# First operands in halves, half a compression block moved, fused sum and extremum, value pages placed and ordered anew

## The reference

```python
# layer 0: S5 state space mixer (48 groups of 64 complex states); layer 1: native sparse attention (NSA)
h = rmsnorm(x, norm_mix_pre[i])
z = h @ w_in                                          # memory queries are columns of z
mkv = mem @ w_mem_kv[i]                               # prompt's 256 memory tokens; samples have a cache
m = concat(mixer(z), mem_attention(z[..., memory], mkv))
x = x + rmsnorm(m @ w_out[i], norm_mix_post[i])
g, u = split(rmsnorm(x, norm_ffn_pre[i]) @ w_ffn_in[i])
x = x + rmsnorm((silu(g) * u) @ w_ffn_out[i], norm_ffn_post[i])
# S5: abar = exp(lam * dt); bu = ug @ bbar; h = scan(abar, bu); y = gelu(c @ h + d * u); y *= sigmoid(y @ w_glu + b)
# NSA compressed keys and values, for the samples out of 8 x 16 pages of 128 rows:
hid = proj[:, :-1, :, 0] + proj[:, 1:, :, 1] + bias   # two overlapping halves of blocks of 32
ckv = gelu(hid) @ w2
# each branch (compressed, selected blocks, window):
s = q @ k * 0.125 - slope[head] * distance            # masked where distance < 0
o = softmax(s) @ v                                    # o = sum of gate * o over the three branches
```

## Time and profile before

| what | value |
|---|---|
| runs, median (lowest to highest of 3) | 1156.15 us (1154.6 to 1156.6) |
| the profiled execution's own time | 1155.58 us |
| its span, first to last instruction | 1153.9 us |
| mean granted TensorE clock | 0.971 of full speed |
| TensorE, VectorE, ScalarE, GpSimd busy | 1079.0, 364.9, 201.8, 245.1 us |
| moved by transfers | 185.20 MB, mean 160 GB/s |

### The profile page before, as it was taken

How to read it: one execution, slowest core, us unless ns; L and a number is a source line. 1 busy time by engine, 2 the same in 40 slices (tenths; PEclk the granted TensorE clock), 3 DMA queues, 4 the chain that set the end, 5 groups by cost and what they waited for, 6 DMA issues and landing times.

```text
span 1153.9 us, 16960 instructions
## 1 busy us (share of the span) xinstructions
PE 1079.0 (94%) x6364; PEld 790.5 (69%) x6364; DVE 364.9 (32%) x783; ACT 201.8 (17%) x496; POOL 245.1 (21%) x314
## 2 busy tenths in 40 slices
PE   6999999999989999999999999785588999999996
PEld 5766666666767777777786776344466777777774
DVE  5629766630142111100023135895014211110002
ACT  3420001002231000010013132664013100000000
POOL 0608756730001101100000022257300110110000
PEclk9999999999989999999999999897698999999998
DMA  8827333431425656675343246368822444343431
GB/s 324 354 76 259 115 110 114 124 93 37 154 73 183 250 204 224 243 280 201 127 170 128 74 143 197 111 178 314 278 74 74 145 146 133 125 144 101 142 134 66
DMA packets 59118, 185.20 MB, mean 160 GB/s; under 512 B 8609, under 2 KB 39586, under 8 KB 48418
## 3 DMA queue, kind: packets, MB, share of 16 engines
q1 hardware_dynamic: 52322, 165.28, 41.3%
q0 software_dynamic: 6144, 12.59, 3.5%
q10 hardware_dynamic: 576, 6.29, 1.4%
HBM read 180.35 MB, written 10.02 MB: 165 GB/s over the span
## 4 chain that ended last, share of the span: by engine, by line
PE 87%; SPq 6%; issue 3%; DVE 2%; DMA 1%; ACT 0%; DVEq 0%
PE banks L731 30%; PE banks L509 16%; PE banks L771 15%; PE banks L707 15%; SPq L416 3%; PE banks L529 3%; SPq L412 2%; PE banks L677 1%; SPq L395 1%; PE banks L1115 1%; PE banks L690 1%; PE banks L575 1%; PE banks L863 1%; PE banks L484 1%; DMA slabs<-in_w 1%
## 5 line engine op out<-in xcount | busy, mean ns | idle before, releaser
L731 PE MATMUL banks<-normed,slabs 128*128 128x288 f32 x1408 | 347.1, 410 | 9.1 <-ACT normed L1224 9.1
L731 PEld LDWEIGHTS banks<-normed,slabs 128*128 128x128 f32 x1408 | 270.5, 192 | 85.5 <-issue 10.0
L771 PE MATMUL banks<-hidden,slabs 128*128 128x288 f32 x704 | 171.2, 406 | 1.5 <-issue 1.5
L707 PE MATMUL banks<-arena,phase 128*128 128x384 f32 x512 | 170.7, 490 | 0.0
L771 PEld LDWEIGHTS banks<-hidden,slabs 128*128 128x128 f32 x704 | 133.6, 190 | 39.1 <-issue 2.4
L707 PEld LDWEIGHTS banks<-arena,phase 128*128 128x128 f32 x512 | 95.5, 190 | 63.2 <-issue 0.2
L1520 POOL TENSOR_TENSOR projected<-projected,rstd 128x288 f32<-128x288 f32 x44 | 34.9, 793 | 440.8 <-ACT projected L1291 440.8
L509 PE MATMUL banks<-normed,slabs 128*128 128x288 f32 (+1 forms) x416 | 107.7, 411 | 1.2 <-ACT normed L1224 1.2
L509 PEld LDWEIGHTS banks<-normed,slabs 128*128 128x128 f32 (+1 forms) x416 | 75.5, 187 | 26.3 <-ACT normed L1224 3.2
L1606 DVE TENSOR_TENSOR normed<-normed 128x288 f32<-128x288 f32 x24 | 11.0, 459 | 199.0 <-ACT normed L1284 199.0
L1291 ACT ACTIVATE projected<-projected 128x288 f32<-128x288 f32 x44 | 19.5, 443 | 281.4 <-DVE projected L1653 281.4
(11 more groups left out here) (300 smaller groups left out, 1060.9 us busy)
## 6 DMA issues: line engine op xcount, KB each, us to landing
slabs<-in_wfi SPq DMA_DIRECT2D x44, 1024.0 KB, 4.9
slabs<-in_w SPq DMA_DIRECT2D x25, 1024.0 KB, 4.8
arena<-in_cmp SPq DMA_DIRECT2D x128, 192.0 KB, 2.8
slabs<-in_wfo SPq DMA_DIRECT2D x32, 704.0 KB, 4.0
arena<-in_slck POOLq DMA_DIRECT2D x64, 96.0 KB, 3.1
arena<-in_slck SPq DMA_DIRECT2D x64, 96.0 KB, 3.4
out_win_old<-in_winold SPq DMA_DIRECT2D x8, 762.0 KB, 6.4
arena<-in_slcv SPq DMA_DIRECT2D x48, 96.0 KB, 4.2
```

The costliest lines, as they stand in the source:

```text
L707: ins = nc.tensor.matmul(out.rearrange("p h (g s) -> p h g s", s=8), W1S[:, c, a, j, :], PG[b % 2][:, :, c * 8 + j, :, :].rearrange("p g h ...
L731: return nc.tensor.matmul(BK[2 * (u % SLOTS) + c][:, 0:T], wt[:, k, c * P:c * P + P], Hn[:, k, :], start=(k == 0), stop=(k == KC - 1), ski ...
L771: ins = nc.tensor.matmul(BK[b][:, 0:T], wt[:, k, :], HD[:, 11 * kh + k, :], start=(kh + k == 0), stop=(kh * 11 + k == 21))
```

## The change

- **First operands.** The memory tokens and the first slab are issued as two halves each, first halves first and ahead of the constants; TensorE starts on the first halves. VectorE does layer 0's sum of squares, norm and normed tiles ahead of the last three angle steps.
- **Compression.** The last value block is cut: 8 of its products stay, 8 go behind `post_sum(1)`. ScalarE copies the sums in layer 0 and takes their Gelu in layer 1 (`last_hidden`), and `compress_v(7)` goes to `beside_in(10)`. The last `s5_y` stands behind the block.
- **Units.** The prompt's queries are scaled by 0.125 / slope in `in_evac` (two instructions instead of one), so that sum and extremum are one `tensor_tensor_reduce`, with the sign turned. The prompt's compressed scores use the same form, and their own maxima are taken as before.
- **Value pages.** The window's tensors move within `slabs`; sequence 6 goes to `projected`, sequence 7 to `slabs`, half by SP and half by GpSimd, which reads all its 16 numbers. On SP the window values come ahead of the number reads, and the first output slab behind `f = 0`, the others behind `f = 1`.

```diff
 # TensorE
-                compress(b, c, between=lambda i: beside_block(blk, i))
+                compress(b, c, between=lambda i: beside_block(blk, i), products=range(8 if blk == 2 * B - 1 else 16))
...
-                    if n < N_UNIT - 1:
-                        s5_y(n)
+                    s5_y(n)
...
-            compress_v(B - 1)
...
             post_sum(1)
+            compress(B - 1, 1, products=range(8, 16))
             channel_mixer(0)
...
+                if i == 10:
+                    compress_v(B - 1)
...
+                    pe.wait_ge(vpage_loaded[b], 16 * (NPG if b < B - 1 else NPG // 2))
+                if f:
+                    pe.wait_ge(vpage_loaded[B], 16 * NPG // 2)
 # ScalarE
+            def last_hidden(half):
+                key = ("hc", B - 1, 1)
+                if half == 0:
+                    banks.take(act, key)
+                    banks.wait_given(act, ("cv", B - 2))
+                    src = BK[6][:, 0:387].rearrange("p (h n) -> p h n", n=129)[:, :, 1:1 + NCMP]
+                    banks.give(A(HCMP[1].rearrange("p (h n) -> p h n", h=H), src, ACT.Copy), key)
+                else:
+                    banks.wait_given(act, key)
+                    A(HCMP[1], HCMP[1], ACT.Gelu_apprx_tanh, bias=CB[:, 1:2]).then_inc(hid_done, 1)
...
             scaled(2)
+            last_hidden(0)
             channel_mixer(0)
...
                     act.wait_ge(state_stored, 32)
+                    last_hidden(1)
...
-                            ins = A(s, s, ACT.Exp, bias=NM[n % 2][:, j:j + 1], accum_out=RS[n % 2][:, j:j + 1])
+                            ins = A(s, s, ACT.Exp, bias=NM[n % 2][:, j:j + 1], scale=-1.0, accum_out=RS[n % 2][:, j:j + 1])
 # VectorE
+                if m < 6:
+                    dve.wait_ge(cst2_loaded, 16)
+                    ch.step(stt(Z[:, m, 0:TP], src[:, 0:TP], c2("qs")[:, m:m + 1], RST[:, 0:TP], ALU.mult, ALU.mult))
+                    ins = stt(Z[:, m, TP:T], src[:, TP:T], 0.125, RST[:, TP:T], ALU.mult, ALU.mult)
+                elif m < 17:
...
+            sum_squares(0, Z[:, 9, :], [Z[:, 9 + k, :] for k in range(1, KC)])
             shape = [P, SC, SEG]
             dve.wait_ge(cst_loaded, 16)
             ch.step(tt(SIN, U1.unsqueeze(2).to_broadcast(shape), c1("tau").unsqueeze(1).to_broadcast(shape), ALU.mult))
+            dve.wait_ge(x_loaded, 16)
+            inverse_root(0)
+            for k in range(KC):
+                stt(Hn[:, k, :], X[:, k, :], norm_g[:, 0, k:k + 1], RST[:, :], ALU.mult, ALU.mult).then_inc(h_done, 1)
             ch.step(ts(COS, SIN, MAGIC, MAGIC, ALU.add, ALU.subtract))
             ch.step(tt(SIN, SIN, COS, ALU.subtract))
             stt(COS, SIN, 0.25, SIN, ALU.is_gt, ALU.subtract).then_inc(trig_arg, 1)
-            dve.wait_ge(x_loaded, 16)
-            pre_norm(0)
-            for k in range(KC):
-                stt(Hn[:, k, :], X[:, k, :], norm_g[:, 0, k:k + 1], RST[:, :], ALU.mult, ALU.mult).then_inc(h_done, 1)
...
-                            ins = stt(SCP[:, :, hd, :], cd, slopes[hd], v[:, :, h, gg, :], ALU.mult, ALU.add)
+                            n = 6 * par + 2 * h + gg
+                            ins = V.tensor_tensor_reduce(SCP[:, :, hd, :], v[:, :, h, gg, :], cd, slopes[hd], NEG, ALU.add, ALU.max,
+                                                         CMX[:, n:n + 1])
...
-                for par in range(2):
-                    banks.take(dve, ("us", n, par))
-                    banks.give(stt(s[:, par, :], c2("causal"), slopes[4 * h + 2 * gg + par], BK[2 * (n % 2) + par][:, 0:3 * P],
-                                   ALU.mult, ALU.add), ("us", n, par))
-                for par in range(2):
-                    banks.wait_given(dve, ("us", n, par))
-                ch.step(V.tensor_reduce(NM[n % 2][:, 0:2], s[:, :, 0:P], AX_X, ALU.max, negate=True))
-                V.tensor_reduce(NM[n % 2][:, 2:4], s[:, :, P:3 * P], AX_X, ALU.max, negate=True).then_inc(u_max, 1)
+                for t in range(2):
+                    for par in range(2):
+                        if t == 0:
+                            banks.take(dve, ("us", n, par))
+                        a, b = P * t, P * t + P * (t + 1)
+                        ins = V.tensor_tensor_reduce(s[:, par, a:b], BK[2 * (n % 2) + par][:, a:b], c2("causal")[:, a:b],
+                                                     -slopes[4 * h + 2 * gg + par], -NEG, ALU.add, ALU.min,
+                                                     NM[n % 2][:, 2 * t + par:2 * t + par + 1])
+                        if t:
+                            banks.give(ins, ("us", n, par))
+                        else:
+                            ch.tick(ins)
+                    if t == 0:
+                        ch.sync()
 # GpSimd
-            for b in (0, 1, 3, 6):
-                numbers = value_numbers(POOL, b)
+            numbers = [value_numbers(POOL, b) for b in (0, 1, 3)]
+            for b, pages in zip((0, 1, 3), numbers):
                 wait_value_slot(pool, b)
-                load_value_pages(pool, b, numbers)
+                load_value_pages(pool, b, pages)
+            numbers = value_numbers(POOL, 6)
+            wait_value_slot(pool, 6)
+            load_value_pages(pool, 6, numbers)
+            numbers = value_numbers(POOL, 7)
+            wait_value_slot(pool, 7)
+            load_value_pages(pool, 7, numbers, range(NPG // 2, NPG), at_=B)
 # SP
+            sp.dma_start(M_[:, 0:4 * NMEM], mem_in[:, 0:4 * NMEM]).then_inc(first_half, 16)
+            sp.dma_start(W_[:, 0:4 * 256], w8_in[0][:, 0:4 * 256]).then_inc(first_half, 16)
+            sp.dma_start(M_[:, 4 * NMEM:KC * NMEM], mem_in[:, 4 * NMEM:KC * NMEM]).then_inc(memt_loaded, 16)
+            sp.dma_start(W_[:, 4 * 256:SLAB], w8_in[0][:, 4 * 256:SLAB]).then_inc(slab_loaded[0], 16)
             sp.dma_start(CS[:, :], cst1_in).then_inc(cst_loaded, 16)
-            sp.dma_start(M_[:, 0:KC * NMEM], mem_in).then_inc(memt_loaded, 16)
-            load(FIRST["mem", 0])
...
-            banks.take(sp, ("hc", B - 1, 1))
+            banks.take(sp, ("hc", B - 1, 0))
...
+            banks.take(sp, ("hc", B - 1, 1))
...
-            numbers = {b: value_numbers(SP, b) for b in (2, 4, 5)}
             banks.take(sp, ("sk", 2, H - 1))
             sp.dma_start(AR[:, 0:6144], winv_in).then_inc(winv_loaded, 16)
-            for b in (2, 4, 5, 7):
-                wait_value_slot(sp, b)
-                load_value_pages(sp, b, numbers[b])
-                if b == 2:
-                    numbers[7] = value_numbers(SP, 7)
-                if b == 4:
-                    load(FIRST["out", 1])
+            numbers = [value_numbers(SP, b) for b in (2, 4)]
+            wait_value_slot(sp, 2)
+            load_value_pages(sp, 2, numbers[0])
+            numbers.append(value_numbers(SP, 5))
+            wait_value_slot(sp, 4)
+            load_value_pages(sp, 4, numbers[1])
+            load_value_pages(sp, 5, numbers[2])
+            numbers = value_numbers(SP, 7)
+            load_value_pages(sp, 7, numbers, range(NPG // 2))
             sp.wait_ge(pair_used, 1)
+            load(FIRST["out", 1])
+            sp.wait_ge(pair_used, 2)
             for u in range(1, N_OUT_SLAB):
                 load(FIRST["out", 1] + u)
```

More of the change, by code:

```diff
@@ L412, in load_key_pages, with load_value_pages @@
                 eng.dma_start(AR[lo:lo + 64, a:a + 384], page(slck_in, r)).then_inc(kpage_loaded[c % 2][parity], 16)
-        def load_value_pages(eng, b, numbers):
-            for n, r in enumerate(numbers):
-                eng.dma_start(VAL[b][:, 192 * n:192 * n + 192], page(slcv_in, r)).then_inc(vpage_loaded[b], 16)
+        def load_value_pages(eng, b, numbers, which=range(NPG), at_=None):
+            for n in which:
+                r = numbers[n]
+                eng.dma_start(VAL[b][:, 192 * n:192 * n + 192], page(slcv_in, r)).then_inc(vpage_loaded[b if at_ is None else at_], 16)
         def wait_value_slot(eng, b):
@@ L425, in wait_value_slot @@
                 eng.wait_ge(cmp_used, 1)
-            elif b < 6:
+            elif b == 6:
+                eng.wait_ge(kv_stored, 16)
+                for j3 in range(2):
+                    banks.take(eng, ("vn", j3))
+            else:
                 eng.wait_ge(win_used, 1)
-            else:
-                banks.take(eng, ("st", NPG))
         released = {}
@@ L693, in s5_y, with compress @@
                 ins.then_inc(y_full, 1)
-            def compress(b, c, between):
+            def compress(b, c, between=lambda i: None, products=range(16)):
                 key = ("hc", b, c)
[L699 to L710, removed]
+                if products[0] == 0:
+                    banks.fill(pe, key, 5 + c)
+                    if c == 0:
+                        pe.wait_ge(page_loaded[b % 2], 16 * NPG * (b // 2 + 1))
+                for i in products:
+                    a, j = i // 8, i % 8
+                    if i:
+                        between(i)
```

(9 more changed lines are left out.)

64 lines of the change are left out of this document (39 added, 25 removed).

## The result

The changed kernel takes 1147.62 us (median of 4 runs, 1147.46 to 1148.18) where the kernel before takes 1156.15: a ratio of 0.993 with a 95% interval of 0.9915 to 0.9946. The profiled execution spans 1146.1 us, 7.8 less than the earlier trace rows.

A forecast was written before the change was run, and what follows sets the result against it. TensorE, busy 1079.0 of 1153.9 us, was taken as the bound, with time won only where it idles or clocks low. Terms -0.8 - 6.4 + 2.5 = -4.7 gave 1151.4 us from 1156.15; range 1145 to 1156, the forecast's own 1147 to 1154.

The forecast's parts named there:

- first operands: Start: halved operands start TensorE 3.0 us earlier, late sines take most back; -0.8, bounds -1.4 and +1.3.
- half block, ahead of glu: Layer 0, compression block to glu: 7.2 us left of 13.25, so -6.05.
- half block, behind the norm: Layer 0: moved products fill 4.57 us of idle, mixer runs at 2.4 GHz; -1.2, bounds +0.9 and -2.1.
- last value product, projection: Layer 1's input projection: the last value product goes where TensorE has no gap, +0.88.
- units, queue shift, value pages: Layer 1's page loads: both queues shift by -1.1, GpSimd's added reads and issues delay the last page; +2.5, bounds 0 and +6.
- Rival C: Behind layer 0's norm: TensorE falls to 1.2 GHz although it has the products; sum -2.6, 1153.5; chance 0.10.
- The dearer evacuations and prompt scores: Projection and prompt scores: at most some 0.3 us dearer each, covered by TensorE's products; nothing, or 3.6 us uncovered.
- Unit maximum: Layer 1's unit loop on VectorE: fused sum and maximum takes 2.0 us for 2.25, 0.25 less a unit.
- Rival D: Unit maxima: fused reduction on a bank is dear, deciding from 0.7 us each; at 1.0, +6.9, 1163; chance 0.08.
- Value pages: Page queues: SP ends 5.8 earlier, near 821.3; GpSimd's last page releases the second half at 829.6 for 827.13, +2.5.
- rival A: Page queues: GpSimd's number reads overlap issues, SP's end decides; -5.8 in place of +2.5, sum -13.0, 1143; chance 0.10.
- Rival B: Page queues: GpSimd issues at its slow rate, pages +6.4, sum -0.8, 1155.3, no change told; chance 0.10.

The follow-up runs named there:

- the kernel before with that line alone: Output slabs 1 to 3 issued behind the second half of the page products, not the first, against the kernel before: ratio 0.9983, 2.0 us faster.
- the start's order alone: The changed kernel with VectorE's angle steps ahead of layer 0's norm again, the halved first operands kept: ratio 0.9939 to the kernel before.
- with the eighth sequence on SP: The changed kernel with all 16 value pages of the eighth sequence on SP, none on GpSimd: 1142.12 us, ratio 0.9882 to the kernel before.
- with the work split anew: The changed kernel with the old start, early number reads, output slab 0 held, 11 eighth-sequence pages on GpSimd and 5 on SP: 1139.24 us, ratio 0.9858.
- with the slab held: The changed kernel with early page-number reads on GpSimd, output slab 0 also waiting for GpSimd's last pages: 1142.26 us, ratio 0.9875 to the kernel before.
- start undone and early numbers: The changed kernel with the start as before and GpSimd reading page numbers early, in its idle time: 1145.55 us, ratio 0.9901 to the kernel before.
- the repeated kernel: The changed kernel run again unedited, on the chip of the last three runs: 1148.01 us (1146.48 to 1149.87), ratio 0.9932 to the kernel before.

## Why the prediction was right, point by point

The direction, the range and the likeliest case held; 1147.6 is inside the forecast's own range of 1147 to 1154, at its lower end. Part of that is luck: the first operands came out 3.1 us worse than summed, and the stretch behind the pages, which is in no term, 5.5 better. The terms of the sum alone measured -2.3, which would have been some 1153.9. Measured by the two timelines (us, minus is faster):

| step of the prediction | predicted | measured | at |
|---|---|---|---|
| first operands | -0.8 | +2.27 | last block's start, 267.29 for 265.02 |
| half block, ahead of glu | -6.05 | -5.91 | glu, 274.63 for 278.27 |
| half block, behind the norm | -1.2 | -1.71 | mixer's first 64 end, 345.30 for 350.65 |
| last value product, projection | +0.88 | +0.62 | layer 1's attention, 711.41 for 716.14 |
| units, queue shift, value pages | +2.5 | +2.44 | second half, 824.98 for 827.27 |
| behind the pages | none | -5.5 | end of the span |
| sum | -4.7 | -7.8 | |

*First operands* is the term with the wrong sign, outside its bounds. The step that failed is "from the fourth microsecond on the queue moves some 0.41 MB in a microsecond": the halves moved at about half that rate, so TensorE was 1.0 us ahead at the norm sum (20.24 for 21.21) and not 3.0. The rest of the argument holds from there: the stall ahead of the scores, 1.65 in the forecast, was 1.61, and the scores came 2.06 later than forecast, as the lead was 2.0 smaller. What VectorE's later work takes ahead of the softmax was too small: 0.55 (from 1.35 to 0.8), where the turn lost another 1.41 against the scores (2.12 late for 0.71).

*Half a block* is the change's main gain and was sized rightly. Rival C had 0.10: it did not happen. The dearer evacuations and prompt scores, costed at nothing, cost nothing that shows: layer 1's projection is +0.62 with the last product in it.

*Unit maximum* was mis-sized: 0.95 us a unit, not 0.25. I took the fixed part of 0.20 from an instruction of 2048 columns and a wait between the two pairs; on a bank the fused form takes 0.28 and 0.42 us, and the next instruction begins 0.21 and 0.35 after its start. The estimate of 1.6 from the Trainium skill ("VectorE: DVE Perf Modes", section "The TRN2 errata"), which I put aside, was nearer to the 1.22 measured than my 2.0. Rival D is out.

*Value pages* came out right by two errors that cancel. The queue shift was 2.57 (743.03 for 750.33, less the 4.73 that TensorE was ahead), not 1.1; and the numbers of the eighth sequence took 6.37, not 4.7. SP's end was far off without a consequence here: forecast 5.8 earlier, measured 15.1, of which 4.73 is TensorE's lead. Its page issues began at 767.75 for 777.77: the key pages ahead ended 5.6 earlier (755.22 for 760.79), and the numbers of two sequences were read first and not of three. So the -5.8 that rival A had from SP's end was priced too low. That GpSimd's last page releases the second half, "near 829 less what the earlier parts won", holds: 824.98 and 4.73 are 829.7. Rival A's condition, number reads hidden beside issues, did not come about by itself; with reads and pages placed for it, the slab held and the start as before, the kernel gains 8.8 us more (1139.24 for 1148.01). Rival B did not happen: GpSimd's groups of 16 took 8.66 to 10.17 in the changed kernel, under the 10.98 that it needs. The rows point the way of a lock-out of GpSimd by VectorE, as the Trainium skill has it ("SBUF — State Buffer", section "Who interferes with whom"), but don't settle it: two groups beside VectorE's work took 10.17 and 10.09, one beside an idle VectorE 8.66, another beside a nearly idle one 9.66.

*Not in the sum*: the change holds three output slabs until the page products are done. I weighed only the first slab's move, and that for the pages only. It takes away the stops: 3.3 us here, 3.0 in the kernel before with that line alone. The other 2.1 goes with the clock: the output projection ran 31.28 for 32.96, with a granted clock of 1.00 in its first 8 us for 0.79, and the next 64 instructions 18.11 for 18.56. The first can't be put down to the change, since among the fourteen profiles eight show 31.28 and six 32.66 to 32.96, without regard to what was edited (the start's order alone, for one). Whether the timed gain holds all of it stays open.

## What to carry to other kernels

A move that takes work out of one place and fills an idle stretch of TensorE with it paid twice here, once where it stood and once in the clock. Where two queues load serially, add up each queue's reads and issues to its end, move reads into the queue's own idle time, and look at what else is being transferred in the last microseconds, for the last small pages landed 4.6 us later beside a large slab. When a first operand is cut to start earlier, follow the whole path to the next wait: here 1.0 us of lead was won, and the angles moved behind the norm lost more than that; with the angles ahead, the later parameters did.

## What I had not expected

Beside the transfers of 1 MB slabs TensorE stopped though it waited for no data of theirs (3.0 us in 11.9), and the landing of a small page took 7.0 us for 2.4. The faster kernels seem to pay the first as well: where output slab 0 is issued beside the second half (at 814.82, 815.12 and 820.37, with the eighth sequence on SP, with the work split anew, and with the slab held) the half takes 9.74, 9.75 and 10.02 us for 8.65.

The granted clock falls in some executions in the midst of work. Behind 48 short instructions (15 columns each) in layer 1's projection one tile takes 5.84 us for 4.15; windows (columns as in the earlier trace rows) of the kernel with start undone and early numbers, then of the changed kernel:

```profile
678.00:680.00 2.00, 2.00 (x6) 1.45 (x5) 1.86 (x25) 0.00 (x0) 1.64 (x5) 0.53 0.62 169
680.00:682.00 2.00, 2.00 (x6) 1.40 (x5) 0.53 (x1) 0.50 (x1) 1.73 (x4) 0.62 0.77 231
```

```profile
678.00:680.00 2.00, 2.00 (x23) 1.76 (x22) 0.84 (x13) 0.00 (x0) 1.79 (x4) 1.00 0.73 258
```

TensorE is busy throughout in both. Five of the fourteen profiles show it, at 1.3 to 3.0 us each on that tile. Together with the output projection's 1.4 to 1.7 it is as large as the scatter of the times (3.4 us in the repeated kernel), and larger than what some of these experiments were to tell apart. That the scatter comes from these two is not shown.
